# Reordering the transposes of normalized tiles at the end of two output projections, and moving a small parameter copy into an earlier stage

## The chip, the cores and the metric

The kernel runs on one core of one Trainium2 chip. The metric is the device time of one launch, in microseconds (us), as the median of several launches; less is better. The core has five engines, each with its own instruction queue, worked off in order: TensorE (PE, matrix products and transposes), VectorE (DVE), ScalarE (ACT), GpSimd (POOL) and SyncE (SP, which issues nearly all DMAs). They wait for one another only by semaphores.

## The reference, cut to what matters

One sequence of 1024 tokens with 1024 features in float32 goes through two blocks.

```
x = layer_norm(x, ln0)                                     # first block
h = x * (1 + sc_a) + sh_a
y = concat(gated delta rule, gated linear attention)(h) @ w_o
x = layer_norm(ALPHA * x + (1 + gt_a) * y, ln1)            # (A)
h = x * (1 + sc_f) + sh_f
u = causal depthwise conv of 3 taps (h @ w_up) + bias
y = (silu(gate half of u) * value half of u) @ w_down
x = layer_norm(ALPHA * x + (1 + gt_f) * y, ln2)
                                                           # second block
h = x + concat(attention, recurrence)(rmsnorm(x)) @ w_out
h = h + cross_attention(rmsnorm(h)) @ w_co
hid = square(relu(rmsnorm(h) @ w_mlp_in))                  # (B)
out = rmsnorm(h + hid @ w_mlp_out)
```

The change concerns the two places (A) and (B): between the product with `w_o` and the feed-forward, and between the product with `w_co` and the MLP.

## The kernel before, in words

Tokens are cut into 8 tiles of 128 (tile 0 to 7), features into 8 chunks of 128. The function `schedule` (lines 270 to 704) writes one list of steps. Each engine's program walks through this one list and issues its own part of each step, so the list sets the order on every engine at once.

**Output projections.** `grouped_products` multiplies attention output by `w_o` (or `w_co`) for three groups of token tiles, (0,1,2,3), (4,5) and (6,7) (`GROUPS`). A group goes through the panels of the weight, each 256 rows by 512 columns: eight panels for `w_o`, numbered 0 to 7, and four for `w_co`, numbered 0 to 3. Sums stand in the PSUM banks that `GROUP_BANKS` gives. The dictionary `between` is the table that the change edits: the entry (g, n) holds steps that follow panel n of group g. VectorE takes each finished bank: at (A) it multiplies by a gate row and adds to the residual (L1764, L1767), at (B) it adds (L1781).

**Normalization.** `norm_start` computes the statistics of a group: at (A) by VectorE alone (`moments` and `deviation`, L1592 to L1620), at (B) by ScalarE's squares (L2358) and then VectorE's reciprocal root by Newton steps (L1614 to L1620). `norm_apply` writes the normalized tile into one of four buffers `xhat0` to `xhat3` (VectorE L1635 at (A), ScalarE L2367 at (B)). In the kernel these are the lists `a1`, `a2`, `a3` for the three groups.

**Turns.** `norm_features` turns normalized tiles into features-by-tokens: TensorE transposes (L1120) into a PSUM bank, one bank for a chunk, and the bank is emptied into a high part and a low part of the float32 values, which the products of the next stage use. At (A): VectorE scales (L1675) into `feat_part`, ScalarE makes `ft_hi` (L2335), and VectorE (even chunks, L1687) or GpSimd (odd chunks, L2754) makes `ft_lo`. There are only two `feat_part` buffers. At (B): ScalarE makes `ftm_hi` (L2344) and VectorE `ftm_lo` (L1667) straight from the bank. Lists `f1`, `f2`, `f3` hold these steps for the three groups, each entry of a list for two chunks; the third argument of `feats` is the ring of banks that it takes in turn. A transpose waits until its bank has been emptied.

**Around (A).** `rows((4, 5))` multiplies normalized tiles by the gain row (VectorE L1650), after which GpSimd adds the bias row (L2745). Behind group 2 come `ffn_taps` (two copies of convolution parameters and two memsets on VectorE, L1984 to L1989), the `late` steps (the last gate vector: eight products L1096 on TensorE, each with a weight panel of its own), the split of the first three `w_up` panels into high (ACT L2291) and low part (POOL L2679), then `f3`, and then the products of the feed-forward (L1127). ScalarE's first split waits for `rows_applied` of tile 5, since `panel_hi` lies over `xhat0` and `xhat1`:

```
            a.wait_ge(*a.filled("feat", 1, 4, KD - 1))
            a.wait_ge("rows_applied", 1, 5)
```

**Around (B).** `first_panels` splits the first two `w_mlp_in` panels; the MLP begins with columns 0 and 1 for the first half of the tokens, then does all of `f3`, and goes on with column 2.

**Panels.** SyncE loads weight panels of 512 KB into six buffers in list order; a load waits until the buffer's last product is done.

Of the kernel before, what the change touches and what calls it, by code (L numbers as in the profile page):

```python
# [308 lines left out]
def schedule(k):  # L309
# [65 lines left out]
    steps = in_turn([[("delta", n, s) for s in DELTA_STEPS] for n in range(NT)], DELTA_LAG)  # L375
# [9 lines left out]
    for m, (_, n, s) in enumerate(steps):  # L385
        for what in delta_banks(s):
            k.banks.take(("delta", n, *what), (5,) if what == ("o",) else (0, 1, 2, 3, 4))
        k.unit("delta", n, s)
        upto = len(fill) * (m + 1) // len(steps)
        for more in fill[done:upto]:  # L390
            for step in more:
                step()
        done = upto
    k.unit("modulation", 1)
    k.unit("resid_load")
# [12 lines left out]
    def feats(s, tiles, ring):  # L408
        return [lambda c=c: norm_features(k, s, tiles, ring, (c, c + 1)) for c in range(0, KD, 2)]

    def applies(s, tiles):
        return [lambda n=n: norm_apply(k, s, n, tiles) for n in tiles]

    def rows(tiles):
        return [lambda n=n: k.unit("norm_scale_rows", 1, n) for n in tiles]
# [3 lines left out]
    f2, a2 = feats(1, (4, 5), (4, 5)), applies(1, (4, 5))  # L419
    f3, a3 = feats(1, (6, 7), (4, 5)), applies(1, (6, 7))  # L420
    grouped_products(k, "w_o", d["w_o"][0], 8, {
        (0, 7): [lambda: norm_start(k, 1, (0, 1, 2, 3)), *a1],
        (1, 2): f1[0:1], (1, 3): f1[1:2], (1, 4): [f1[2], *rows((0, 1))], (1, 5): [f1[3], *rows((2, 3))],
        (1, 7): [lambda: norm_start(k, 1, (4, 5)), *a2],
        (2, 2): f2[0:1], (2, 3): f2[1:2], (2, 4): f2[2:3], (2, 5): [f2[3], *rows((4, 5))],
        (2, 7): [lambda: norm_start(k, 1, (6, 7)), *a3]})
    w_up, w_down = d["ffn_w_up"][0], d["ffn_w_down"][0]
# [12 lines left out]

    k.unit("ffn_taps")
    for step in late:
# [37 lines left out]
    ring = (4, 5, 6, 7)  # L480
# [121 lines left out]
    ring = (4, 5)  # L602
# [48 lines left out]
    f1, a1 = feats("norm_mlp", (0, 1, 2, 3), ring), applies("norm_mlp", (0, 1, 2, 3))  # L651
    f2, a2 = feats("norm_mlp", (4, 5), ring), applies("norm_mlp", (4, 5))
    f3, a3 = feats("norm_mlp", (6, 7), ring), applies("norm_mlp", (6, 7))
    w_mi, w_mo = d["w_mlp_in_2"][0], d["w_mlp_out_2"][0]
    first_in = []

    def first_panels():
# [4 lines left out]
        (0, 3): [lambda: norm_start(k, "norm_mlp", (0, 1, 2, 3)), *a1],  # L662
        (1, 3): [lambda: norm_start(k, "norm_mlp", (4, 5)), f1[0], f1[1], first_panels],
        (2, 0): f1[2:3], (2, 1): [f1[3], *a2],
        (2, 3): [lambda: norm_start(k, "norm_mlp", (6, 7)), f2[0], f2[1], f2[2], f2[3], *a3]},
        resident=True)
# [857 lines left out]
def vector_program(k):  # L1524
# [458 lines left out]
    def ffn_taps():  # L1983
        dve.tensor_copy(k.ffn_taps[:, :, :, 0:3],  # L1984
                        k.col("ffn_conv", 0, 3 * 2 * NFF).rearrange("p (j g c) -> p g c j", j=3, g=2))
        dve.tensor_copy(k.ffn_taps[:, :, :, 3:4],
                        k.col("ffn_conv_b", 0, 2 * NFF).rearrange("p (g c j) -> p g c j", g=2, j=1))
        for n in range(2):
            m = dve.memset(k.ffn_in[n][:, 0:3], 0.0)  # L1989
        m.then_inc(*v.new("ffn_ready"))  # L1990
# [260 lines left out]
    def mlp_out(i, u, h, p, tiles):  # L2251
        for n in tiles:
            v.wait_ge(*v.filled("mlp_out", i, u, h, n))
            if u or i:
# [7 lines left out]
               norm_features=norm_features, final=final, project=project, to_tokens=to_tokens, decay_gates=decay_gates,  # L2262
               delta_start=delta_start, delta=delta, gla_gates=gla_gates, gla=gla, ffn_taps=ffn_taps, up=up, down=down,
               rg_params=rg_params, rg_in=rg_in, rglru=rglru, angles=angles, masks=masks, score=score, weigh=weigh, merge=merge,
# [822 lines left out]
```

## Time and profile before

| | us |
|---|---|
| median of 3 launches | 3224.68 |
| lowest and highest | 3221.36, 3225.28 |
| launch that was profiled | 3222.75 |
| its span in the trace | 3221.5 |
| TensorE busy in it | 3040.6 |
| VectorE busy | 1491.2 |
| ScalarE busy | 938.2 |
| GpSimd busy | 773.7 |

The launch takes 1.25 us more than the span. Times inside the span count from its start. A row of the timeline reads: start, length, engine, line of the kernel, operation, output and inputs, count; in square brackets how long the engine had been idle before it, and what it waited for.

### The profile page before, as it was taken

The numbers are of one execution on the slowest core, as the hardware profiler recorded it, in microseconds if no ns is written. First come the engines' busy times: TensorE is split into PE (matmuls) and PEld (weight loads), VectorE is DVE, ScalarE is ACT, GpSimd is POOL, SyncE is SP. The second block draws the span as 40 slices with busy tenths as digits, with TensorE's granted clock in tenths as the row PEclk, the third lists the DMA queues.
The fourth block names the chain that finished last, engine by engine and source line by source line (L and its number), as shares of the span: only waits on it lengthen the run. The fifth ranks groups of instructions, "written<-read, shape, count | busy, mean of one in ns | idle before, by whom it ended". The sixth has DMA issues, their size and how long they took to land.

```text
span 3221.5 us, 32486 instructions
## 1 busy us (share of the span) xinstructions
PE 3040.6 (94%) x13068; PEld 2167.0 (67%) x13068; DVE 1491.2 (46%) x2375; ACT 938.2 (29%) x1476; POOL 773.7 (24%) x481
## 2 busy tenths in 40 slices
PE   6999999999979999999997899999998999999997
PEld 3444467675437888888875668785444788888886
DVE  7235443332475554545556564662233333333334
ACT  1236632223012222222224541362243222222123
POOL 3111112211044444444430333111000222222221
PEclk9999999999989999999998999999999999999998
DMA  7210012213231111111113112102201111111111
GB/s 250 66 33 27 27 40 73 65 40 111 87 122 46 60 51 46 46 51 48 46 53 111 33 40 81 60 3 98 93 27 33 39 46 53 46 47 52 46 53 53
DMA packets 199749, 193.55 MB, mean 60 GB/s; under 512 B 16152, under 2 KB 147632, under 8 KB 199600
## 3 DMA queue, kind: packets, MB, share of 16 engines
q1 hardware_dynamic: 197968, 187.09, 18.5%
q10 hardware_dynamic: 1631, 4.40, 0.4%
q8 instruction: 104, 1.70, 0.2%
q14 instruction: 46, 0.37, 0.0%
HBM read 175.43 MB, written 13.89 MB: 59 GB/s over the span
## 4 chain that ended last, share of the span: by engine, by line
PE 82%; DVE 8%; ACT 6%; issue 2%; POOL 1%; DMA 1%; ACTq 0%; SPq 0%; DVEq 0%; POOLq 0%
PE bank L1127 60%; PE bank L1154 6%; PE bank L1450 2%; PE bank L1220 1%; PE bank L1261 1%; PE bank L1120 1%; PE bank L1275 1%; PE bank L1284 1%; PE bank L1434 1%; PE bank L1404 1%; PE bank L1426 1%; PE bank L1096 1%; DVE ffn_conv L2005 1%; DVE ffn_conv L2001 1%; PE bank L1423 1%
## 5 line engine op out<-in xcount | busy, mean ns | idle before, releaser
L1127 PE MATMUL bank<-ft_hi,panel_lo 128*128 128x512 f32 x1216 | 443.8, 398 | 27.9 <-POOL panel_lo L2679 27.9
L2679 POOL TENSOR_TENSOR panel_lo<-panel,panelm_hi 128x1024 fp32r<-128x1024 f32 x64 | 153.3, 2396 | 813.2 <-ACT panelm_hi L2291 813.2
L1127 PEld LDWEIGHTS bank<-ft_hi,panel_lo 128*128 128x128 f32 x1216 | 232.6, 191 | 81.0 <-POOL panel_lo L2679 29.6
L1154 PE MATMUL bank<-ft,panel 128*128 128x512 f32 x576 | 271.5, 609 | 7.4 <-ACT mod_part L2398 4.8
L1127 PE MATMUL bank<-ft_hi,panel_hi 128*128 128x512 f32 x704 | 276.8, 393 | 0.0
L1127 PE MATMUL bank<-ft_lo,panel_hi 128*128 128x512 f32 x704 | 276.4, 393 | 0.0
L2001 DVE TENSOR_SCALAR ffn_conv<-ffn_in,ffn_taps 128x512 f32<-128x512 f32 x88 | 115.5, 1312 | 296.6 <-ACT ffn_in L2538 296.6
L2257 DVE TENSOR_TENSOR resid<-resid,bank 128x512 f32<-128x512 f32 x256 | 174.7, 687 | 151.3 <-PE bank L1127 150.5
L2679 POOL TENSOR_TENSOR panel_lo<-panel,panel_hi 128x1024 fp32r<-128x1024 f32 x66 | 158.5, 2409 | 246.6 <-ACT panel_hi L2291 246.6
L1127 PE MATMUL bank<-ftm_hi,panelm_hi 128*128 128x512 f32 x512 | 201.1, 393 | 0.0
L1127 PE MATMUL bank<-ftm_hi,panel_lo 128*128 128x512 f32 x512 | 200.6, 392 | 0.0
L1127 PE MATMUL bank<-ftm_lo,panelm_hi 128*128 128x512 f32 x512 | 200.6, 392 | 0.0
L1127 PE MATMUL bank<-panelm_hi,mlp_hid_hi 128*128 128x512 f32 x512 | 199.2, 389 | 0.0
L1127 PE MATMUL bank<-panel_lo,mlp_hid_hi 128*128 128x512 f32 x512 | 199.2, 389 | 0.0
L1127 PE MATMUL bank<-panelm_hi,mlp_hid_lo 128*128 128x512 f32 x512 | 199.2, 389 | 0.0
L1154 PEld LDWEIGHTS bank<-ft,panel 128*128 128x128 f32 x576 | 105.3, 194 | 113.9 <-issue 110.7
L1127 PE MATMUL bank<-panel,mix 128*128 128x512 f32 x384 | 169.4, 598 | 2.9 <-DMA panel<-in_w_out 2.0
L2005 DVE SCALAR_TENSOR_TENSOR ffn_conv<-ffn_in,ffn_taps,ffn_conv 128x512 f32<-128x512 f32 x176 | 156.5, 889 | 6.2
L2244 DVE TENSOR_TENSOR mlp_square<-mlp_act 128x512 f32<-128x512 f32 x64 | 44.3, 692 | 236.7 <-ACT mlp_act L2641 236.7
L1127 PEld LDWEIGHTS bank<-ft_lo,panel_hi 128*128 128x128 f32 x704 | 132.7, 189 | 30.9
L1127 PEld LDWEIGHTS bank<-ft_hi,panel_hi 128*128 128x128 f32 x704 | 132.6, 188 | 29.6
L1127 PE MATMUL bank<-panel_hi,ffn_hid_hi 128*128 128x512 f32 x352 | 140.0, 398 | 9.4 <-POOL ffn_hid_lo L2824 6.9
(430 smaller groups left out, 5574.1 us busy)
## 6 DMA issues: line engine op xcount, KB each, us to landing
panel<-in_w_in SPq DMA_DIRECT2D x52, 512.0 KB, 3.7
panel<-in_w_ada SPq DMA_DIRECT2D x48, 512.0 KB, 3.8
panel<-in_ffn_w_up SPq DMA_DIRECT2D x44, 512.0 KB, 3.7
panel<-in_w_mlp_in SPq DMA_DIRECT2D x32, 512.0 KB, 3.9
panel<-in_w_mlp_out SPq DMA_DIRECT2D x32, 512.0 KB, 3.5
panel<-in_w_o SPq DMA_DIRECT2D x24, 512.0 KB, 3.6
panel<-in_w_out SPq DMA_DIRECT2D x24, 512.0 KB, 3.5
panel<-in_ffn_w_down SPq DMA_DIRECT2D x22, 512.0 KB, 3.6
```

The costliest lines, as they stand in the source:

```text
L1096: m = te.matmul(ps[rows, :], k.cond[:, c:c + 1].broadcast_to([P, 32]), w[:, kk, :], start=(c < 4), stop=(c >= 4))
L1120: m = te.transpose(ps[:, tile(i)], src[:, tile(j)], k.ident[:])
L1127: m = te.matmul(ps, a, b, start=(start and j == 0), stop=(stop and j == len(pairs) - 1))
L1154: m = te.matmul(ps[:], w[0][:, kk, :], k.ft[:, kk, half(h)], start=(kk == 0), stop=(kk == KD - 1))
L1220: m = te.matmul(ps[:, tile(h)], lhs(h), rhs_of(h), start=True, stop=True)
L1261: m = te.matmul(ps[:, h * GC:(h + 1) * GC], t.ltm[:, h, :], blocks(t.inv, lv, 0)[:, h], start=True, stop=True)
L1450: m = te.matmul(ps[:, at:at + HD + 1], k.p_t[(2 * t + hb) % 4][:, 2 * side + c, :], v, start=(hb == side == c == 0), stop=(hb == side == c ...
L2001: dve.tensor_scalar(out, pre[:, 1 + h * BANK:1 + (h + 1) * BANK], w[:, 0:1], w[:, 3:4], ALU.mult, ALU.add).then_inc(*v.new("ffn_tap", c, g ...
L2005: dve.scalar_tensor_tensor(out, pre[:, 1 + j + h * BANK:1 + j + (h + 1) * BANK], w[:, j:j + 1], out, ALU.mult, ALU.add).then_inc(*v.new("f ...
L2244: dve.tensor_tensor(k.mlp_sq[h][:], k.mlp_act[h][:], k.mlp_act[h][:], ALU.mult).then_inc(*v.new("mlp_square", i, c, h))
L2257: evict(dve.tensor_tensor(r, r, v.bank("mlp_out", i, u, h, n)[:], ALU.add), "mlp_out", i, u, h, n)
L2679: pool.tensor_tensor(lo, k.view(p), hi.bitcast(F32), ALU.subtract).then_inc(*g.new("halved_lo", p))
```

## The change

The steps stay the same; their places in the list, the banks of some, and the place of one copy change.

- (A), group 2 (tiles 6 and 7): the four steps of `f2` (the turns of tiles 4 and 5) stood behind panels 2, 3, 4 and 5, and now stand behind 4, 5 and 6 (two steps behind 6). `rows((4, 5))` stood behind panel 5 and now stands behind `a3`, the normalization of tiles 6 and 7.
- (A), `f3`: eight banks in turn in place of banks 4 and 5.
- (A), the two copies into `ffn_taps` are made in the middle of the delta rule; the two memsets stay, as `ffn_edges`.
- (B), group 1: the first two steps of `f1` stood behind panel 3 and behind the statistics of tiles 4 and 5; now the first stands behind panel 2, the second behind panel 3 and ahead of those statistics.
- (B), group 2: `f2` stood behind panel 3 and behind the statistics of tiles 6 and 7; now two steps stand behind panel 2 and two behind panel 3, ahead of those statistics. Its ring has four banks in place of two, `f3` has eight.

```diff
+        if m == len(steps) // 2:
+            k.unit("ffn_taps")
...
-    f3, a3 = feats(1, (6, 7), (4, 5)), applies(1, (6, 7))
+    f3, a3 = feats(1, (6, 7), tuple(range(8))), applies(1, (6, 7))
...
-        (2, 2): f2[0:1], (2, 3): f2[1:2], (2, 4): f2[2:3], (2, 5): [f2[3], *rows((4, 5))],
-        (2, 7): [lambda: norm_start(k, 1, (6, 7)), *a3]})
+        (2, 4): f2[0:1], (2, 5): f2[1:2], (2, 6): f2[2:4],
+        (2, 7): [lambda: norm_start(k, 1, (6, 7)), *a3, *rows((4, 5))]})
...
-    k.unit("ffn_taps")
+    k.unit("ffn_edges")
...
-    f2, a2 = feats("norm_mlp", (4, 5), ring), applies("norm_mlp", (4, 5))
-    f3, a3 = feats("norm_mlp", (6, 7), ring), applies("norm_mlp", (6, 7))
+    f2, a2 = feats("norm_mlp", (4, 5), (2, 3, 4, 5)), applies("norm_mlp", (4, 5))
+    f3, a3 = feats("norm_mlp", (6, 7), tuple(range(8))), applies("norm_mlp", (6, 7))
...
-        (1, 3): [lambda: norm_start(k, "norm_mlp", (4, 5)), f1[0], f1[1], first_panels],
-        (2, 0): f1[2:3], (2, 1): [f1[3], *a2],
-        (2, 3): [lambda: norm_start(k, "norm_mlp", (6, 7)), f2[0], f2[1], f2[2], f2[3], *a3]},
+        (1, 2): f1[0:1], (1, 3): [f1[1], lambda: norm_start(k, "norm_mlp", (4, 5)), first_panels],
+        (2, 0): f1[2:3], (2, 1): [f1[3], *a2], (2, 2): f2[0:2],
+        (2, 3): [f2[2], f2[3], lambda: norm_start(k, "norm_mlp", (6, 7)), *a3]},
```

On TensorE in group 2 of the product with `w_o`, the order before was this (`mixed` and `g_v` hold attention output, `xhat0` and `xhat1` the normalized tiles 4 and 5, `ident` the identity; a panel shows as two banks, two products each):

```order
L1127 MATMUL bank6<-panel0_79,mixed_90 128x512 x2
L1127 MATMUL bank7<-panel0_79,mixed_90 128x512 x2
L1120 MATMUL bank4<-ident_49,xhat0_153 128x128
L1120 MATMUL bank4<-ident_49,xhat1_154 128x128
L1120 MATMUL bank5<-ident_49,xhat0_153 128x128
L1120 MATMUL bank5<-ident_49,xhat1_154 128x128
L1127 MATMUL bank0<-panel1_80,mixed_90 128x512 x2
```

In the changed kernel, from the same panel on:

```order
L1129 MATMUL bank6<-panel0_79,mixed_90 128x512 x2
L1129 MATMUL bank7<-panel0_79,mixed_90 128x512 x2
L1129 MATMUL bank0<-panel1_80,mixed_90 128x512 x2
L1129 MATMUL bank1<-panel1_80,mixed_90 128x512 x2
L1129 MATMUL bank6<-panel2_81,g_v_92 128x512 x2
L1129 MATMUL bank7<-panel2_81,g_v_92 128x512 x2
L1122 MATMUL bank4<-ident_49,xhat0_153 128x128
L1122 MATMUL bank4<-ident_49,xhat1_154 128x128
```

Two panels now stand between the second panel-half and the first transpose of tile 4.

On VectorE behind the normalization of tiles 6 and 7 (`xhat_155`, `xhat_156`) at (A), before:

```order
L1635 TENSOR_SCALAR xhat_155<-resid,moments,rstd 128x1024
L1635 TENSOR_SCALAR xhat_156<-resid,moments,rstd 128x1024
L1984 COPY ffn_taps<-cols 128x44x3
L1986 COPY ffn_taps<-cols 128x44
L1989 MEMSET ffn_in_170 128x3
L1989 MEMSET ffn_in_171 128x3
L1561 SCALAR_TENSOR_TENSOR gate_row<-bank,gate_row 128x512 x2
L1675 TENSOR_SCALAR feat_part_157<-bank,in_scale,in_bias 128x256
```

and in the changed kernel:

```order
L1637 TENSOR_SCALAR xhat_155<-resid,moments,rstd 128x1024
L1637 TENSOR_SCALAR xhat_156<-resid,moments,rstd 128x1024
L1652 TENSOR_TENSOR resid<-xhat_153,norm_rows 128x1024
L1652 TENSOR_TENSOR resid<-xhat_154,norm_rows 128x1024
L1993 MEMSET ffn_in_170 128x3
L1993 MEMSET ffn_in_171 128x3
L1563 SCALAR_TENSOR_TENSOR gate_row<-bank,gate_row 128x512 x2
L1677 TENSOR_SCALAR feat_part_157<-bank,in_scale,in_bias 128x256
```

The two copies are gone from here, and the rows of tiles 4 and 5 have come in their place.

On ScalarE at (B), behind the normalization of tiles 0 to 3 (`square` are the squares of tiles 4 and 5, `panelm_hi` the split of the MLP's first panels), before:

```order
L2367 ACTIVATE xhat3_156<-resid2_205,rstd_61 128x1024
L2358 ACTIVATE square_159,moments_60<-resid2_205 128x1024 x2
L2344 ACTIVATE ftm_hi_238<-bank4,cols_52 128x512
L2344 ACTIVATE ftm_hi_238<-bank5,cols_52 128x512
L2344 ACTIVATE ftm_hi_238<-bank4,cols_52 128x512
L2344 ACTIVATE ftm_hi_238<-bank5,cols_52 128x512
L2291 ACTIVATE panelm_hi0_248<-panel0_79 128x1024
```

and in the changed kernel:

```order
L2371 ACTIVATE xhat3_156<-resid2_205,rstd_61 128x1024
L2348 ACTIVATE ftm_hi_238<-bank4,cols_52 128x512
L2348 ACTIVATE ftm_hi_238<-bank5,cols_52 128x512
L2348 ACTIVATE ftm_hi_238<-bank4,cols_52 128x512
L2348 ACTIVATE ftm_hi_238<-bank5,cols_52 128x512
L2362 ACTIVATE square_159,moments_60<-resid2_205 128x1024 x2
L2295 ACTIVATE panelm_hi0_248<-panel0_79 128x1024
```

The squares, and VectorE's Newton steps that wait for them, now stand behind the first four chunks.

## Rows read from the trace of the kernel before

**Rows 1.** The page: chain that ended last, share of the span by engine.

```profile
PE 82%; DVE 8%; ACT 6%; issue 2%; POOL 1%; DMA 1%; ACTq 0%; SPq 0%; DVEq 0%; POOLq 0%
```

**Rows 2.** Chain that ended last, in order of time: start, us, what.

```profile
954.65 18.63 PE bank L1127 x72
...
1025.81 620.60 PE bank L1127 x2688
...
2515.08 676.45 PE bank L1127 x2976
```

**Rows 3.** Waits of TensorE at (A): line, waited for, total, times, longest.

```profile
PE bank L1120 <- DVE xhat L1635: 7.2, 6, 5.7
PE bank L1120 <- DVE feat_part L1675: 6.0, 4, 5.1
```

**Rows 4.** Timeline of TensorE at (A), 897 to 955 us.

```profile
897.39 5.42 PE L1127 MATMUL bank<-panel,mixed 128*128 128x512 f32 x12 [0.70 <-DVE gated L1764]
908.54 0.45 PE L1120 MATMUL bank<-ident,xhat 128*128 128x128 f32 x1 [5.73 <-DVE xhat L1635]
...
916.08 3.60 PE L1127 MATMUL bank<-panel,g_v 128*128 128x512 f32 x8
...
919.95 3.60 PE L1127 MATMUL bank<-panel,g_v 128*128 128x512 f32 x8
...
930.78 2.77 PE L1096 MATMUL bank<-panel,cond 128*32 128x512 f32 x20
...
941.76 1.99 PE L1108 MATMUL bank<-mod_last,quads 128*128 128x512 f32 x2 [0.74 <-ACT mod_last L2398]
...
954.30 0.78 PE L1127 MATMUL bank<-ft_hi,panel_hi 128*128 128x512 f32 x1
```

**Rows 5.** Timeline of VectorE at (A), 925 to 948 us.

```profile
925.17 2.88 DVE L1650 TENSOR_TENSOR resid<-xhat,norm_rows 128x1024 f32<-128x1024 f32 x2
...
928.70 2.12 DVE L1767 TENSOR_TENSOR resid<-resid,gated 128x512 f32<-128x512 f32 x1
...
936.57 1.28 DVE L1592 BATCH_NORM_STATS2 stats<-resid 128x6 f32<-128x512 f32 x2
...
941.89 1.53 DVE L1635 TENSOR_SCALAR xhat<-resid,moments,rstd 128x1024 f32<-128x1024 f32 x2
943.34 2.39 DVE L1984 COPY ffn_taps<-cols 128x132 f32<-128x132 f32 x1
945.65 2.35 DVE L1986 COPY ffn_taps<-cols 128x44 f32<-128x44 f32 x1
```

**Rows 6.** Timeline of GpSimd at (A), 926 to 951 us.

```profile
926.94 6.11 POOL L2745 TENSOR_TENSOR resid<-resid,norm_rows 128x1024 f32<-128x1024 f32 x2
942.74 7.50 POOL L2679 TENSOR_TENSOR panel_lo<-panel,panel_hi 128x1024 fp32r<-128x1024 f32 x3 [9.69 <-ACT panel_hi L2291]
```

**Rows 7.** Timeline of VectorE in the delta rule, around 612 us.

```profile
611.97 0.69 DVE L1895 TENSOR_TENSOR rhs<-bank,g_col 128x512 f32<-128x512 f32 x1 [2.61 <-PE bank L1220]
```

**Rows 8.** Waits of TensorE, 2400 to 2560 us.

```profile
PE bank L1120 <- DVE ftm_lo L1667: 14.5, 7, 4.5
```

**Rows 9.** Timeline of TensorE at (B).

```profile
2465.45 1.97 PE L1120 MATMUL bank<-ident,xhat 128*128 128x128 f32 x8 [4.30 <-DVE ftm_lo L1667]
...
2489.68 1.11 PE L1120 MATMUL bank<-ident,xhat 128*128 128x128 f32 x4 [4.47 <-DVE ftm_lo L1667]
```

**Rows 10.** Chain that ended last, at (B).

```profile
2472.72 0.88 PE bank L1120 x8
2473.59 3.44 PE bank L1127 x8
...
2494.48 12.80 PE bank L1127 x48
```

**Rows 11.** Timeline of ScalarE at (B).

```profile
2450.93 4.27 ACT L2367 ACTIVATE xhat<-resid,rstd 128x1024 f32<-128x1024 f32 x4 [2.42 <-DVE rstd L1620]
...
2522.43 0.60 ACT L2641 ACTIVATE mlp_act<-bank 128x512 f32<-128x512 f32 x1 [6.84 <-PE bank L1127]
```

More of the change, by code:

```diff
@@ L1987, in ffn_taps, with ffn_edges @@
                         k.col("ffn_conv_b", 0, 2 * NFF).rearrange("p (g c j) -> p g c j", g=2, j=1))
+    def ffn_edges():
         for n in range(2):
@@ L2262, in vector_program @@
                norm_features=norm_features, final=final, project=project, to_tokens=to_tokens, decay_gates=decay_gates,
-               delta_start=delta_start, delta=delta, gla_gates=gla_gates, gla=gla, ffn_taps=ffn_taps, up=up, down=down,
+               delta_start=delta_start, delta=delta, gla_gates=gla_gates, gla=gla, ffn_taps=ffn_taps, ffn_edges=ffn_edges, up=up, down=down,
                rg_params=rg_params, rg_in=rg_in, rglru=rglru, angles=angles, masks=masks, score=score, weigh=weigh, merge=merge,
```

## The prediction

> **What bounds the kernel now.** I read the chain that ended last first, since it says which engine's work a microsecond must be taken from. TensorE holds 82% of it [rows 1], so the kernel gets shorter where TensorE waits, or where it runs slowly behind a wait. In order of time the chain shows two long stretches on which nothing but products lie, 620.60 us from 1025.81 and 676.45 us from 2515.08 [rows 2]. What comes ahead of each is a seam: (A), from the product with `w_o` to 1025.81, and (B), from the product with `w_co` to 2515.08. The waits then say what TensorE lacks there. At (A) its transposes wait 7.2 us for normalized tiles (one wait of 5.7) and 6.0 us for the emptying of banks 4 and 5 (one of 5.1) [rows 3]; at (B) they wait 14.5 us for the emptying of the same two banks, 4.5 the longest [rows 8]. The timelines place them: 5.73 us ahead of 908.54, 4.30 ahead of 2465.45, 4.47 ahead of 2489.68 [rows 4, 9]. Work behind a wait is slower too: at 2489.68 four transposes take 1.11 us, and the first feed-forward product takes 0.78 us [rows 4, 9]; in the stretches of rows 2 one product takes 620.60 / 2688 = 0.231 us.
>
> **(A), group 2 on TensorE.** The second and third panel of the group end at 897.39 + 5.42 = 902.81, then comes the wait of 5.73 for tiles 4 and 5 and the group ends at 930.78 [rows 4]. Five panels were left. In the changed kernel two of them stand ahead of the first transpose, 2 x 3.44 us, until 909.7; the normalized tiles come at about 909.1 as before, so the wait goes. A panel and its four transposes take 919.95 - 916.08 = 3.87 us [rows 4]: 5 x 3.44 + 4 x 0.43 = 18.9 us. One gap is new. The last two steps of `f2` stand together, and their two banks are emptied only after VectorE has done two tiles of panel 6 (four operations of 0.7 us, begun during the panel); I put it at 1.6 us. The group ends at 902.8 + 20.5 = 923.3, 7.5 us earlier.
>
> **(A), VectorE.** Now the statistics of tiles 6 and 7 begin at 936.57, 5.8 us behind the group's end, since `rows((4, 5))` (2.88 us) goes ahead and its partner on GpSimd (6.11 us for two) slows the first additions behind it from 0.7 to 2.12 us [rows 5, 6]. With the rows moved behind, I count on VectorE from the end of panel 6 (917.5): two tiles 1.4 more us, the last four chunks of `f2` to 922.6, and four operations on the last two tiles, the last of which starts 1.2 us behind the group's end: statistics at 925.6, 11.0 us earlier. From there the start of the feed-forward follows from a chain on VectorE and GpSimd: 943.42 - 936.57 = 6.85 us until both tiles are normalized, 1.44 until the row of tile 4 is done, 6.1 for the two additions on GpSimd (with VectorE's operations between), 2.5 for the first low part of a `w_up` panel (7.50 / 3) [rows 5, 6]. Sum 16.9, so 942.5 against 954.30 [rows 4], 11.8 us. The other things that this product needs come earlier: the late gate vector's last product on TensorE ended at 943.75, 13.0 us behind the group's end [rows 4], so now at 936.3, and the eight banks let all of `f3`'s transposes follow it in 2 us. I take off 0.8 for a stretch at half clock that the new gap of 1.6 us may bring (it would cost 8 x 0.2 us): **11 us**, between 8 and 13.
>
> The rest of `f3` gains less. GpSimd makes three low parts ahead of its share of `f3`: they end at 942.5 + 2 x 2.5 = 947.5 against 942.74 + 7.50 = 950.24 now [rows 6], so `f3` ends only 2.7 us earlier. Its end now is near 957, by four pairs of chunks at 1.7 us behind 950.24 (two features, a low part on each engine), so 954.5 in the changed kernel. The third unit of the feed-forward is the first to use it. Three units took from 954.30 to 954.65 + 18.63 = 973.3 [rows 2, 4], the third 24 x 0.231 = 5.5, so it starts 13.5 us behind the first, at 956. I see `f3` covered, but the cover is thin: 1.5 us. The chain passes through the end of this third unit [rows 2], which shifts with TensorE.
>
> **The copies.** They take 2.39 and 2.35 us now, for 132 and 44 elements, while GpSimd makes three low parts in 7.50 us [rows 5, 6]; 44 elements cannot cost as much as 132 by their own work, so it is the waiting for GpSimd that I read there. In the delta rule they stand ahead of two operations that end a 2.61 us idle time before [rows 7]. Between nothing and 4.7 us, I take 0.5 us of VectorE work and nothing on the path. If that cover were gone, 2.1 us would be lost. The Trainium skill says in "SBUF — State Buffer", section "SBUF: two separate sides", that VectorE and GpSimd hold a shared port pair exclusively for a whole instruction; the trace agrees with the 2.39 and 2.12 us. It speaks against moving the rows next to the splits: were the two engines free of each other, the 6.1 us would be about 4.5 and the start 1.5 us earlier, and that is no term of the sum.
>
> **(B).** TensorE has ended panel 3 of group 1 and eight transposes at 2465.45 - 4.30 = 2461.15, so panel 2 at 2461.15 - 0.88 - 3.44 = 2456.8 [rows 9, 10]. Tiles 0 to 3 are normalized at 2455.2 [rows 11], so the first turn no longer waits. What is left until the first MLP product is five panels of 3.44, four pairs of chunks of four tiles at 0.88, and four pairs of two tiles at 0.43 [rows 10]: 17.2 + 3.5 + 1.7 = 22.4, which gives 2479.2 against 2494.48 [rows 10]: 15.3 us. For this ScalarE must keep step. From 2461.5, when the second pair of chunks is turned, it has two high parts, two squares, two splits, four high parts and two normalizations ahead of the turn of tiles 4 and 5: six operations over 1024 elements at 4.27 / 4 = 1.07 us and six over 512 at 0.60 to 0.70 [rows 11], 10.0 to 10.6 us, and some 1.5 us in which it waits for TensorE's fourth pair. That ends near 2473.6, and the transposes are due at 2456.8 + 17.2 = 2474.0: 0.4 us of room.
>
> Behind it 48 products took 12.80 us [rows 10], and 48 x 0.231 = 11.1 without a wait ahead: 1.6 us. The turns of tiles 6 and 7 took 2507.3 to 2515.08, 7.8 us; on eight banks the 16 transposes need 1.8, and the next unit's bank is empty 1.5 us later: 4.5 us. That unit took until 2522.4 [rows 11], 7.3 us against 24 x 0.231 = 5.6: 1.7 us. Sum 15.3 + 1.6 + 4.5 + 1.7 = **23 us**, between 15 and 25. From there TensorE alone is on the path [rows 2], so all of it counts.
>
> **Sum.** 3222.75 - 11 - 23 = 3188.8 for the profiled launch, which was 1.9 us below the median of the three. I predict 3190.
>
> **Rivals.**
> 1. As above, 3183 to 3195: chance 0.60.
> 2. At (A) the feed-forward's start follows `f3` and the conversions behind it, not TensorE: only 3 us are gained there. For it: the cover of 1.5 us. Against it: the chain now runs through TensorE's first three units, 18.63 us without a gap [rows 2], not through `f3`. 3222.75 - 3 - 23 = 3197: 0.13.
> 3. At (B) ScalarE comes late for tiles 4 and 5, and a wait like that of 2465.45 returns: 4.3 us, and 3.0 us of slow work behind it (2472.72 - 2465.45 = 7.3 for what takes 0.88 + 3.44 at full speed [rows 9, 10]). For it: 0.4 us of room. 3189 + 7 = 3196: 0.14.
> 4. The turns wait all the same, now for other banks or for panels, and the two seams keep their length: 3220 to 3224. Against it: every load follows a product, so loads move with TensorE. 0.05.
> 5. Slower: the transposes now stand in closer company and TensorE is granted half clock for long behind them. A product then costs 0.2 us more (0.43 against 0.231); the forecast's 34 us are used up after 170 such products, seven units at the feed-forward's start, and past 200 it is slower. Against it: behind 954.30 only some ten products were slow. Above 3229: 0.03.
> The last 0.05 lies between these, mostly at smaller gains.
>
> **Numbers.** From 3183 (13 and 25 us) to 3201 holds 1, 2, 3 and a little more: 8 in 10 or above. A measurement of this kernel tells about 0.2%, 6.4 us, from no change. Faster by more: 1, 2, 3 and most of the rest, 0.92; within: 0.05; slower: 0.03.
>
> **What would show it.** Right: no wait of 5.7 us for `xhat` in group 2, statistics of tiles 6 and 7 near 925.6, first feed-forward product near 942.5, the 620 us stretch starting near 1015, first MLP product 15 us earlier in relation to the start of `w_co`'s product, waits of L1120 for `ftm_lo` near 1.5 us in place of 14.5, granted clock 1.00 from 2460 to 2500. Wrong: a wait of L1127 for `ft_lo` or `ftm_hi` at either start, a longer gap on VectorE near 608, or TensorE waiting for `xhat` after panel 2 of group 2 at (B).

## The result and the profile after

The changed kernel took 3196.36 us (median of four launches, 3190.62 to 3199.6), the kernel before 3223.75 beside it (four, 3221.36 to 3225.28): a ratio of 0.9913, 95% interval 0.9901 to 0.9924, or 27.4 us less. The forecast was 3190, from 3183 to 3201. The measured time lies in the range, but 6 us above the forecast, so a term was too large. The launches that were profiled took 3222.75 and 3196.19 us, 26.6 less.

In the rows of after, line numbers are 2 to 4 higher. The chain that ended last shows where the two seams end now, to be held against [rows 2]:

```profile
1012.77 622.76 PE bank L1129 x2688
...
2488.51 676.46 PE bank L1129 x2976
```

The first long stretch of products begins 13.0 us earlier, takes 2.2 us longer, the part between the stretches takes 1.0 us longer, and the last one begins 26.6 us earlier. The product with `w_co` began at 2418.84 and now begins at 2408.99, so 16.7 us of it come from seam (B) and 9.9 are left of (A). The forecast had 11 for (A) and 23 for (B).

**(A).** Waits of TensorE from 905 to 1021 us in the changed kernel, the first three rows (line, waited for, total, times, longest). The waits of 5.7 and 5.1 us in [rows 3] are gone; the largest is new, one for GpSimd:

```profile
PE bank L1129 <- POOL panel_lo L2683: 4.0, 1, 4.0
PE bank L1129 <- ACT ffn_in L2542: 3.5, 2, 3.3
PE bank L1098 <- DMA panel<-in_w_ada: 2.9, 3, 1.2
```

Timeline of TensorE there, answering to [rows 4]:

```profile
895.66 8.85 PE L1129 MATMUL bank<-panel,mixed 128*128 128x512 f32 x20 [0.71 <-DVE gated L1766]
...
917.66 0.89 PE L1122 MATMUL bank<-ident,xhat 128*128 128x128 f32 x4 [1.53 <-DVE feat_part L1677]
918.39 3.60 PE L1129 MATMUL bank<-panel,g_v 128*128 128x512 f32 x8
921.92 2.77 PE L1098 MATMUL bank<-panel,cond 128*32 128x512 f32 x20
...
933.52 2.04 PE L1122 MATMUL bank<-ident,xhat 128*128 128x128 f32 x16
939.58 0.80 PE L1129 MATMUL bank<-ft_hi,panel_hi 128*128 128x512 f32 x1 [4.02 <-POOL panel_lo L2683]
```

The 16 transposes of tiles 6 and 7 stand together. Then TensorE waits 4.02 us for the first low part. Why that is late stands in the timeline of GpSimd:

```profile
931.44 5.60 POOL L2749 TENSOR_TENSOR resid<-resid,norm_rows 128x1024 f32<-128x1024 f32 x2 [10.22 <-DVE resid L1652]
936.99 7.21 POOL L2683 TENSOR_TENSOR panel_lo<-panel,panel_hi 128x1024 fp32r<-128x1024 f32 x3
```

The high parts came from ScalarE at 932.61 to 934.8, but GpSimd first had the two additions for tiles 4 and 5. VectorE, answering to [rows 5]:

```profile
923.36 1.28 DVE L1594 BATCH_NORM_STATS2 stats<-resid 128x6 f32<-128x512 f32 x2
...
928.69 1.53 DVE L1637 TENSOR_SCALAR xhat<-resid,moments,rstd 128x1024 f32<-128x1024 f32 x2
930.14 2.35 DVE L1652 TENSOR_TENSOR resid<-xhat,norm_rows 128x1024 f32<-128x1024 f32 x2
```

The copies, in the delta rule, answering to [rows 7]: 0.23 and 0.20 us in place of 2.39 and 2.35. Idle time still follows them, 2.39 us where it was 2.61.

```profile
608.30 0.23 DVE L1986 COPY ffn_taps<-cols 128x132 f32<-128x132 f32 x1
608.45 0.20 DVE L1988 COPY ffn_taps<-cols 128x44 f32<-128x44 f32 x1
...
611.94 0.69 DVE L1897 TENSOR_TENSOR rhs<-bank,g_col 128x512 f32<-128x512 f32 x1 [2.39 <-PE bank L1222]
```

**(B).** Waits of TensorE, 2380 to 2540 us. The 14.5 us of [rows 8] are gone, and three new waits, 5.8 us in all, have come:

```profile
PE bank L1122 <- DVE ftm_lo L1669: 2.8, 1, 2.8
PE bank L1129 <- DVE ftm_lo L1669: 2.4, 1, 2.4
...
PE bank L1122 <- ACT mlp_act L2645: 0.6, 1, 0.6
```

Their places in the timeline of TensorE: the fourth step of `f1` (the second turn of [rows 9] had waited 4.30 us), the last turn of `f3`, and the third MLP unit.

```profile
2462.71 1.31 PE L1122 MATMUL bank<-ident,xhat 128*128 128x128 f32 x8 [2.79 <-DVE ftm_lo L1669]
...
2485.66 0.44 PE L1122 MATMUL bank<-ident,xhat 128*128 128x128 f32 x2 [0.57 <-ACT mlp_act L2645]
2488.51 0.60 PE L1129 MATMUL bank<-ftm_hi,panelm_hi 128*128 128x512 f32 x1 [2.41 <-DVE ftm_lo L1669]
```

What held the low part up is on VectorE, in the root steps for tiles 4 and 5:

```profile
2456.38 0.16 DVE L1622 SCALAR_TENSOR_TENSOR rstd<-newton,rstd 128x2 f32<-128x2 f32 x1
2456.57 2.21 DVE L1620 SCALAR_TENSOR_TENSOR newton<-rstd 128x2 f32<-128x2 f32 x1
2458.82 2.27 DVE L1621 TENSOR_TENSOR newton<-newton 128x2 f32<-128x2 f32 x1
2461.12 0.16 DVE L1622 SCALAR_TENSOR_TENSOR rstd<-newton,rstd 128x2 f32<-128x2 f32 x1
...
2482.02 2.43 DVE L2248 TENSOR_TENSOR mlp_square<-mlp_act 128x512 f32<-128x512 f32 x1 [3.76 <-ACT mlp_act L2645]
```

Two operations on two elements per partition take 2.2 us where their like take 0.16. GpSimd's timeline has one instruction of 2.35 us beside each, and one beside `mlp_square`:

```profile
2456.37 4.70 POOL L2683 TENSOR_TENSOR panel_lo<-panel,panelm_hi 128x1024 fp32r<-128x1024 f32 x2 [259.62 <-ACT panelm_hi L2295]
2481.52 2.39 POOL L2683 TENSOR_TENSOR panel_lo<-panel,panelm_hi 128x1024 fp32r<-128x1024 f32 x1 [20.46 <-ACT panelm_hi L2295]
```

In the kernel before, GpSimd's first pair of low parts began at 2469.17, after the root steps had ended at 2464.6; now the step of `f1` with its 1.41 us of low parts is queued on VectorE behind them.

### The profile page after: what moved, and what is told of

Its sections match the earlier page's. It is cut to its first block, busy times and chain, and to the rows that moved or that the text cites. A ratio compares the mean times of both kernels' runs of the same rounds, so it can differ in the third digit from the quotient of the medians.

```text
span 3195.0 us, 32486 instructions
## 1 busy us (share of the span) xinstructions
PE 3023.4 (95%) x13068; PEld 2157.7 (68%) x13068; DVE 1488.9 (47%) x2375; ACT 936.3 (29%) x1476; POOL 771.9 (24%) x481
## 4 chain that ended last, share of the span: by engine, by line
PE 82%; DVE 7%; ACT 6%; POOL 2%; issue 1%; DMA 1%; SPq 0%; ACTq 0%; DVEq 0%; POOLq 0%
PE bank L1129 60%; PE bank L1156 6%; PE bank L1452 2%; PE bank L1222 1%; PE bank L1263 1%; PE bank L1277 1%; PE bank L1286 1%; PE bank L1436 1%; PE bank L1406 1%; DVE ffn_conv L2009 1%; PE bank L1428 1%; PE bank L1098 1%; POOL panel_lo L2683 1%; PE bank L1122 1%; PE bank L1425 1%
## 5 line engine op out<-in xcount | busy, mean ns | idle before, releaser
L2005 DVE TENSOR_SCALAR ffn_conv<-ffn_in,ffn_taps 128x512 f32<-128x512 f32 x88 | 114.0, 1295 | 289.5 <-ACT ffn_in L2542 289.5
L1129 PE MATMUL bank<-panel_hi,ffn_hid_hi 128*128 128x512 f32 x352 | 141.6, 402 | 10.9 <-POOL ffn_hid_lo L2828 6.9
```

The lines of the kernel that those rows point to most:

```text
L1129: m = te.matmul(ps, a, b, start=(start and j == 0), stop=(stop and j == len(pairs) - 1))
L2005: dve.tensor_scalar(out, pre[:, 1 + h * BANK:1 + (h + 1) * BANK], w[:, 0:1], w[:, 3:4], ALU.mult, ALU.add).then_inc(*v.new("ffn_tap", c, g ...
```

## The experiments

Since launches of one kernel differ by up to 9 us, I read each experiment in its trace by three distances besides its median. **S**: from the last turn of `f2` at (A) (917.66 in the changed kernel) to the first feed-forward product. **L**: from the same turn to the long product stretch. **B**: from the start of the product with `w_co` to the end of the last product stretch (before: 2515.08 + 676.45 - 2418.84 = 772.7).

| kernel | median | ratio to before, 95% | S | L | B |
|---|---|---|---|---|---|
| changed | 3196.36 | 0.9913 (0.9901, 0.9924) | 21.9 | 95.1 | 756.0 |
| a_only | 3211.26 | 0.9958 (0.9945, 0.9970) | 21.7 | 95.1 | 772.5 |
| b_only | 3207.52 | 0.9945 (0.9932, 0.9957) | | | 757.4 |
| taps_back | 3195.55 | 0.9906 (0.9891, 0.9921) | 22.1 | 95.4 | 757.4 |
| rows_back | 3197.56 | 0.9915 (0.9902, 0.9929) | 27.2 | 97.6 | 756.1 |
| splits_late | 3190.44 | 0.9900 (0.9885, 0.9914) | 21.9 | 95.1 | 749.6 |
| splits_early | 3191.36 | 0.9904 (0.9889, 0.9918) | 21.9 | 95.1 | 752.7 |
| adds_late | 3194.20 | 0.9911 (0.9894, 0.9927) | 18.5 | 94.6 | 756.1 |
| third_bank | 3189.75 | 0.9899 (0.9884, 0.9914) | 21.9 | 95.1 | 751.2 |
| f3a_two | 3200.60 | 0.9931 (0.9917, 0.9944) | 30.1 | 100.6 | 757.4 |
| f3b_two | 3198.84 | 0.9925 (0.9912, 0.9937) | 21.9 | 95.1 | 760.0 |
| best1 | 3186.23 | 0.9887 (0.9873, 0.9900) | 21.7 | 95.1 | 747.8 |
| best2 | 3181.36 | 0.9870 (0.9857, 0.9883) | 18.5 | 91.9 | 747.8 |

S and L stand only for kernels with the new order at (A), since in the old one the last turn of `f2` has another place. Where nothing was changed at the seam, they repeat there within 0.3 us. The old order repeats less well: from the row that ends the wait for `gated` (897.39 in [rows 4], 895.66 in the changed kernel) to the long stretch it is 128.4 us in the kernel before and 129.3 in b_only, and 117.1 in the changed kernel and in a_only. The change at (A) is thus worth 11.3 to 12.2 us up to the long stretch. B takes one of two values where (B) is that of the changed kernel, 756.0 or 757.4: in the second kind the eight transposes behind the wait of 2.9 us took 1.97 us and not 1.31 (granted clock 0.50 from 2470.40 to 2472.40 in b_only, 1.00 from 2462.60 to 2464.00 in the changed kernel).

**The two halves apart.** a_only has the changes at (A) and the copies, b_only those at (B).

> The changes at (A) and the copies alone, (B) as before. Theory (the two seams add up, and what (A) gained is 11.3 us less 1.4 lost in the long product stretch): 10 us under before, about 3213, with the first feed-forward product near 940 and everything from the product with w_co on as in before, shifted. Rival (the gain at (A) is given back in the feed-forward or in the second block when (B) waits as before): within 4 us of before, 3219 or more.

> The changes at (B) alone. Theory (VectorE's small root steps wait for GpSimd's low parts of the first two MLP panels, and that costs the predicted gain its missing part): 16 to 17 us under before, about 3206, with a wait of 2 to 3 us of TensorE for ftm_lo at the fourth turn of group 1 as in the changed kernel. Rival (the shortfall at (B) comes from the other phase in which (A) leaves the loads and the clock): 21 to 23 us under before, about 3200.

Measured: 12.9 and 16.7 us under before (3224.19 beside them). L and B are those of the changed kernel in the half that was changed, and B is that of before in a_only. In b_only TensorE waits 2.94 us for `ftm_lo` at the fourth turn, as expected. The rivals fall: the two seams are independent, and what (B) lacks it lacks by itself.

**The copies.** The unit stands again where it was, behind the rows of tiles 4 and 5:

```diff
-        if m == len(steps) // 2:
-            k.unit("ffn_taps")
...
+    k.unit("ffn_taps")
     k.unit("ffn_edges")
```

> The changed kernel, with the two copies of the convolution parameters back ahead of the two memsets, so behind the rows of tiles 4 and 5 on VectorE and beside GpSimd's additions. Theory: each copy is held until a GpSimd instruction ends, 2.2 to 2.8 us for each, but the first feed-forward product waits for GpSimd's low part and not for VectorE, so the start stays near 939.6 and the time within 2 us of the changed kernel. Rival (the copies were on the path of the start, as the sum of the prediction allowed): the start 4 to 5 us later, time about 3201.

Measured: the first copy took 0.23 us and only the second was held, for 2.40 us, so the theory's "each copy" was wrong. S and L grew by 0.2 us only, and the median is that of the changed kernel. The rest of the theory holds: VectorE's 2.4 us lie in TensorE's wait for GpSimd. Moving the copies is worth next to nothing here.

**The rows of tiles 4 and 5**, ahead of the statistics again:

```diff
-        (2, 4): f2[0:1], (2, 5): f2[1:2], (2, 6): f2[2:4],
-        (2, 7): [lambda: norm_start(k, 1, (6, 7)), *a3, *rows((4, 5))]})
+        (2, 4): f2[0:1], (2, 5): f2[1:2], (2, 6): [*f2[2:4], *rows((4, 5))],
+        (2, 7): [lambda: norm_start(k, 1, (6, 7)), *a3]})
```

> The changed kernel, with the rows of tiles 4 and 5 (VectorE's products and GpSimd's additions) behind the last step of f2 in group 2, ahead of the statistics of tiles 6 and 7. Theory A (rows ahead of the statistics delay the start by 4 us, as the prediction counted): statistics near 927.5, first feed-forward product 2 to 4 us later than 939.6, time 3198 to 3200. Theory B (the start waits for GpSimd's low part, which waits for GpSimd's additions of the rows; with the additions done earlier the low part is ready near 936): first product near 937.5, 2 us earlier, time about 3194, with TensorE waiting for xhat instead.

Measured: the start is 5.2 us later, more than either theory gave. The statistics came at 929.72, 10.9 us behind the last turn and not 5.7, 5.2 us later where theory A counted 4. Behind them the root steps fell beside GpSimd's low parts, which started at 934.28. The timeline of VectorE in rows_back:

```profile
934.45 2.20 DVE L1620 SCALAR_TENSOR_TENSOR newton<-rstd 128x2 f32<-128x2 f32 x1
936.68 2.27 DVE L1621 TENSOR_TENSOR newton<-newton 128x2 f32<-128x2 f32 x1
938.98 2.26 DVE L1622 SCALAR_TENSOR_TENSOR rstd<-newton,rstd 128x2 f32<-128x2 f32 x1
```

GpSimd's low parts did begin earlier, as theory B wanted (15.5 us behind the last turn and not 19.3), but now TensorE waits 7.81 us for `xhat`. Three root steps were held ahead of `xhat`, which is the thing that the forecast missed at (B). Of the 5.2 us, L keeps 2.4. The median moved by 1.2 us, less than launches differ, so this one stands on the trace alone.

**The splits of the first MLP panels**, moved to either side of the root steps. splits_late:

```diff
-        k.unit("ahead", used=first_in[0])
...
-        (2, 0): f1[2:3], (2, 1): [f1[3], *a2], (2, 2): f2[0:2],
+        (2, 0): [f1[2], lambda: k.unit("ahead", used=first_in[0])], (2, 1): [f1[3], *a2], (2, 2): f2[0:2],
```

splits_early:

```diff
-        (1, 2): f1[0:1], (1, 3): [f1[1], lambda: norm_start(k, "norm_mlp", (4, 5)), first_panels],
+        (1, 2): [first_panels, f1[0]], (1, 3): [f1[1], lambda: norm_start(k, "norm_mlp", (4, 5))],
```

> The changed kernel, with the splits of the first MLP panels moved behind the third step of f1 (entry (2, 0)), so that GpSimd's low parts begin after VectorE's small root steps for tiles 4 and 5; the third panel's split comes with them, ahead of the turn of tiles 6 and 7. Theory (the root steps waited for GpSimd's low parts): root steps 2.4 us in all instead of 6.3, no wait of 2.8 us of TensorE for ftm_lo at the fourth turn, first MLP product 2.8 us earlier, and up to 1.4 us more at the third MLP unit, since mlp_square takes 0.7 and not 2.4 us: 3 to 4 us under the changed kernel, about 3192. Rival (ScalarE is what is late: squares, splits and high parts in its queue): now one more split stands ahead of the high parts of the fourth turn, the wait stays or grows to 3 us: 3196 or more.

> The changed kernel, with the splits of the first two MLP panels ahead of the first step of f1 (entry (1, 2)), where ScalarE was idle for 2.1 us, and the loads of the four panels in the same place. GpSimd's low parts then lie from 2446.4 to 2451.1, beside VectorE's additions and low parts, which read a bank, and ahead of the root steps. Theory (only operations of VectorE with both inputs in SBUF wait for GpSimd, as 0.7 us for operations with a bank beside GpSimd's instructions at (A) suggest): no wait at the fourth turn, 2.8 us earlier, about 3193. Rival (operations that read a bank wait for GpSimd too): the low parts of the first step come 2 to 4 us late, TensorE waits at the second turn instead, no gain: 3196.

Measured: B is 6.4 and 3.3 us shorter, the medians 5.9 and 5.0 under the changed kernel. In both, the wait at the fourth turn is gone. splits_late puts three splits ahead of the high parts of that turn on ScalarE and does not wait for them, so ScalarE was not what was late. splits_late gains more since the third panel's split has moved too: `mlp_square` takes 0.69 us and not 2.43, TensorE waits 1.6 us ahead of the third MLP unit and not 2.41 (2.4 in splits_early), and the granted clock from 2490 to 2495 is 1.00 where it was 0.79. The row of VectorE and the wait of TensorE in splits_late:

```profile
2480.41 0.69 DVE L2248 TENSOR_TENSOR mlp_square<-mlp_act 128x512 f32<-128x512 f32 x1 [2.81 <-ACT mlp_act L2645]
```

```profile
PE bank L1129 <- DVE ftm_lo L1669: 1.6, 1, 1.6
```

In splits_early VectorE works beside GpSimd's low parts (row of GpSimd, then two of VectorE):

```profile
2445.04 4.68 POOL L2683 TENSOR_TENSOR panel_lo<-panel,panelm_hi 128x1024 fp32r<-128x1024 f32 x2 [249.32 <-ACT panelm_hi L2295]
```

```profile
2446.95 1.41 DVE L1669 SCALAR_TENSOR_TENSOR ftm_lo<-bank,cols,ftm_hi 128x512 fp32r<-128x512 f32 x2 [0.55 <-ACT ftm_hi L2348]
2448.31 0.69 DVE L1783 TENSOR_TENSOR resid<-resid,bank 128x512 f32<-128x512 f32 x1
```

They take what they take alone, 0.7 us for each: an operation that reads a bank is not held in any of these rows. The rival of splits_early falls. Its theory is too narrow, though. Two inputs in SBUF are not what it takes: the copies of [rows 5] have one, and so have the first convolution steps (`ffn_conv`, L2005 of the changed kernel, a TENSOR_SCALAR of 512 elements with one tap for each partition), which took 0.54 us alone at 952.46 and 2.23 us at 1004.93, where GpSimd had an instruction of 2.39 us from 1004.48. What the held operations have in common is that they read no bank; whether every such operation is held, no run tells.

**The third MLP unit's bank.** third_bank turns the last two chunks of `f3` behind the third unit:

```diff
-                for step in ((), f3, ())[c]:
+                for step in ((), f3[0:3], f3[3:4])[c]:
```

> The changed kernel, with the last step of f3 at (B) (chunks 6 and 7) behind the third MLP unit in place of ahead of it, so that this unit finds an empty bank and needs not wait until f3's first bank is emptied. Theory (the wait of 2.4 us ahead of the third unit is for a bank): that wait goes, and what comes in its place is at most the last two chunks, turned while ScalarE has had 5.5 us: 2 us under the changed kernel, about 3194. Rival (the wait only moves behind the third unit, since f3's high and low parts end no earlier): the fourth unit waits as long, no change, 3196.

Measured: B is 4.8 us shorter, the median 6.6 lower, more than the 2 expected. The wait of 2.4 us is gone and the one of 0.57 for `mlp_act` with it. The rest is the clock: busy time by stretches of 5 us (stretch, length, busy time and instructions of the engines, granted clock PEclk), first the changed kernel, then third_bank.

```profile
2485.00:2490.00 5.00, 2.03 (x7) 1.43 (x7) 4.12 (x9) 4.00 (x11) 0.00 (x0) 0.87 0.00 0
2490.00:2495.00 5.00, 5.00 (x19) 3.97 (x19) 1.10 (x3) 0.15 (x1) 0.00 (x0) 0.79 0.01 3
```

```profile
2485.00:2490.00 5.00, 5.00 (x25) 4.15 (x24) 3.50 (x8) 3.14 (x9) 0.00 (x0) 1.00 0.01 3
2490.00:2495.00 5.00, 5.00 (x23) 4.13 (x22) 1.98 (x4) 1.33 (x3) 0.00 (x0) 1.00 0.03 5
```

Without idle time in front the clock stays at 1.00, and the second stretch holds 23 instructions in place of 19. Idle time need not bring it down either: it stayed at 1.00 behind the 1.6 us of splits_late. The 4.8 us less the 3.0 of the two waits leave 1.8 us, which I put down to the clock.

**GpSimd's additions at (A).** adds_late takes them out of the wait for the first low part:

```diff
-        if n < 6:
+        if n < 4:
             rows_add(s, (n,))
...
-    k.unit("rows_add", 1, (6, 7))
+    k.unit("rows_add", 1, (4, 5))
     for n in range(2):
         up(0, n, first[n], 1)
+    k.unit("rows_add", 1, (6, 7))
```

> The changed kernel, with GpSimd's additions of the bias row to tiles 4 and 5 behind the first two units of the feed-forward, and those to tiles 6 and 7 behind the fourth; VectorE's order is the same. Theory (the first feed-forward product waits for GpSimd's low part, and this for the two additions of 5.6 us, while the high parts are ready at 933.7): low parts from 933.7, first product near 936.3, 3.3 us earlier; 2 to 3 us under the changed kernel, about 3193. Rival (the additions, now beside the first convolutions, hold up VectorE there, as one pair did already with 5.59 us for two operations): the gain is lost again at the units behind, 3196 or more.

Measured: S is 3.4 us shorter, as expected, but L only 0.5, and the ratio to before is no different (0.9911 beside 0.9913). The rival holds. The second pair lies beside VectorE's convolutions at 975.98. In the chain of adds_late two convolution steps are held there, where the changed kernel has 2.78 and 0.76:

```profile
978.70 2.79 DVE ffn_conv L2010
981.51 2.77 DVE ffn_conv L2010
```

The step behind them took 1.37 us for 0.56, so the three account for 2.8 of the 2.9 us that were given back.

**The eight banks, one seam at a time** (f3a_two: `(4, 5)` for `tuple(range(8))` in `f3` at (A); f3b_two: `ring` at (B)).

> The changed kernel, with f3 at (A) on banks 4 and 5 again. Theory (between the start of the feed-forward and the long product stretch the path runs through f3's conversions and VectorE's convolutions, so the eight banks count there): in the kernel before, f3 ended near 957 and in the changed one near 951; with two banks TensorE's transposes also stand ahead of the first product, so that the start follows the emptying: start 4 to 7 us later than in the changed kernel, the long stretch 3 to 6 us later, time 3199 to 3202. Rival (the eight banks do nothing here, since the low part of the panel comes at the same time): start within 1 us of 22 us behind the last turn of group 2, time about 3196.

> The changed kernel, with f3 at (B) on the old ring of two banks. Theory (the prediction's term for the eight banks, 4.5 us, was right): the turns take about 7.8 us in place of the 2.8 until the third unit's wait of 2.4, time 3 to 4.5 us over the changed kernel, about 3200. Rival (ScalarE's high parts set the pace with two banks as with eight): within 1 us of the changed kernel.

Measured: at (A) S grows by 8.2 us and L by 5.5, the median by 4.2; at (B) B grows by 4.0 and the median by 2.5. Both theories hold, with a start that is later than the 4 to 7 us of the first and a median that moved less than the 3 to 4.5 us of the second. Waits of TensorE, first in f3a_two from 905 us, then in f3b_two from 2440 us:

```profile
PE bank L1122 <- DVE feat_part L1677: 11.9, 6, 4.5
```

```profile
PE bank L1122 <- DVE ftm_lo L1669: 8.6, 4, 4.4
```

**Together.** best1 is splits_early with third_bank. best2 adds the additions, the second pair this time behind the first half of the first product with `w_down`:

```diff
                 down(i, h, ps[h], tiles)
+                if i == 0 and h == 0:
+                    k.unit("rows_add", 1, (6, 7))
```

> splits_early and third_bank together. Theory (the wait of 2.9 at the fourth turn and the one of 2.4 ahead of the third MLP unit are apart from each other): both go, 5.3 us under the changed kernel in the trace from the product with w_co to the long MLP stretch; time about 3190 to 3191 beside 3196 for the changed kernel. Rival (they cover each other: the MLP begins earlier, but tiles 6 and 7 are normalized no earlier, so a wait for xhat takes their place): 3192 or more.

> best1, with GpSimd's additions of the bias row to tiles 4 and 5 behind the first two feed-forward units (as in adds_late) and those to tiles 6 and 7 behind the first half of the first product with w_down. In adds_late the start came 3.4 us earlier, and 2.9 of it were given back where the second pair of additions lay beside VectorE's convolutions. Theory (in this stretch VectorE and GpSimd work one after the other, so only work taken out of it counts): the gain of 3 us stays, long stretch 3 us earlier in relation to the last turn of group 2, time 3187 to 3188. Rival (the additions delay GpSimd's low parts of the next panels, or VectorE's emptying of the banks for tiles 6 and 7 waits for them): no gain over best1 or a loss of up to 5 us.

Measured: 3186.23 and 3181.36 us, 10 and 15 under the changed kernel, with intervals of the ratio apart from its own (0.9873 to 0.9900 and 0.9857 to 0.9883 against 0.9901 to 0.9924). At (B) TensorE waits for nothing from 2440 to 2560 in either, and B is 8.2 us shorter: in best1 3.2 up to the first MLP product, as in the two kernels with moved splits, and 4.9 behind it, as in third_bank. That is more than the 5.3 of the two waits, and I put the rest down to the wait of 0.57 and to the clock, as in third_bank. In best2 the first feed-forward product and the pair of additions lie so (TensorE, then GpSimd):

```profile
936.41 0.50 PE L1131 MATMUL bank<-ft_hi,panel_hi 128*128 128x512 f32 x1 [1.05 <-POOL panel_lo L2685]
```

```profile
1013.12 4.77 POOL L2751 TENSOR_TENSOR resid<-resid,norm_rows 128x1024 f32<-128x1024 f32 x2
```

Both S and L are 3.2 to 3.4 us shorter: with the additions behind the start of the long stretch at 1009.80, the gain at the start is kept. The medians of best1 and best2 lie 4.9 us apart, but the intervals of their ratios overlap; the 3.2 us in L are what the traces show.

## Why the prediction was right, and what was off

**(A), 11 us: right.** To compare it with the rows, 1.7 us come off first: the changed kernel was already that much ahead at the row of 895.66 (before: 897.39, [rows 4]), in a part whose order the change doesn't touch. There the granted clock was 0.85 from 866 to 872 us and 0.80 from 872 to 876 before, and 1.00 in both in the changed kernel. Predicted and measured, the latter with 1.7 added:

- End of group 2: 923.3, measured 923.6. The gap of 1.6 us is there, at 1.53.
- Statistics of tiles 6 and 7: 925.6, measured 925.1.
- First product: 942.5, measured 941.3.
- Long stretch: near 1015, measured 1014.5, so 11.3 us earlier (13.0 with the 1.7). Of the 13.0, 9.9 arrive at the start of (B): the stretch itself took 2.2 us more, as in best1 (622.79 for 620.6) and in no other run by more than 0.5, and the part behind it 1.0. That 1.0 is not the change's: from the end of the long stretch to the product with `w_co` it is 772.4 us in the trace of before, and at least 773.3 in every other, b_only with its old (A) among them. So the 9.9 is not the worth of (A): 1.7 us that the clock gave ahead of it are in it, and 3.2 us were lost in parts whose order the change leaves alone.
- The copies: nothing on the path, as predicted.

The working was less right than the sum. It took the start as TensorE's and `f3` as a thing thinly covered. In the chain of the changed kernel, no TensorE work lies between 949.7 and 1011.9 but VectorE's rows and convolutions, with ScalarE's and GpSimd's pieces between them. Where that stretch begins:

```profile
948.84 0.55 DVE feat_part L1677
949.39 0.33 DVE ft_lo L1689
949.72 0.67 DVE resid L1652
```

f3a_two shows that the banks of `f3` alone carry 5.5 us there, which the prediction didn't price at (A). That is the mechanism of rival 2. It took no gain away since `f3` ended 4.7 us earlier and not 2.7 (its last low part on GpSimd began at 949.91 + 1.7 = 951.6, before at 956.34): GpSimd began its own share of `f3` at 944.16 + 1.7 = 945.9, where the prediction had 947.5, and eight banks then let nothing else wait. That (A) came out at 11 is in part luck, then: of the 11.3 us, f3a_two gives 5.5 to the banks, rows_back 2.4 to the place of the rows and taps_back 0.2 to the copies. If these add up, some 3 us are left for the later turns of `f2`, an estimate that no run checks by itself.

**(B), 23 us: 16.7 measured, the term that was mis-sized.**

- 15.3 for the order of the turns, measured 11.9 (first MLP product 2472.40 - 2408.99 = 63.4 us behind the start of the product with `w_co`, before 2494.13 - 2418.84 = 75.3). The step that failed is the condition under this term, "For this ScalarE must keep step", with its 0.4 us of room: it named ScalarE as the only engine that the turns could wait for. ScalarE did keep step. What the sum left out is VectorE's root steps, which the change put beside GpSimd's low parts. In splits_early and in splits_late, without that, the product comes at 60.2 us, and 60.4 was predicted (2479.2 - 2418.84). So the price of the held root steps is 3.2 us, and 1.3 to 1.5 us more where the clock falls behind the wait (64.9 us in b_only, taps_back and f3a_two). Rival 3 had a wait for `ftm_lo` come back, as it did, but for the turns of tiles 4 and 5 and through ScalarE; it was the last turn of tiles 0 to 3, through VectorE. Its 3196 is the measured time by luck.
- 1.6 and 4.5 for the first units and `f3`, measured 4.8 (from the first product to the third unit 20.95 before, 16.1 now). The 1.6 is 12.80 - 11.1, so 1.7 by its own rows. The wait ahead of the third unit was to be 1.5 us and was 0.57 + 2.41, since `mlp_square` was held for 2.43 us; in splits_late, where it was not, that wait is 1.6. The eight banks are worth 4.0, by f3b_two.
- 1.7 for the third unit at full clock, measured 0: it stood behind idle time again, and the clock was 0.87 and 0.79. third_bank gets it.

The Trainium skill says in "SBUF — State Buffer", section "SBUF: two separate sides", that a VectorE operation with two inputs in SBUF, against a GpSimd instruction that reads SBUF, or one in a 2-port performance mode, can't run beside GpSimd, and that whichever starts first keeps the ports for its whole length. The rows agree for 2.21, 2.27 and 2.43 us, for the 0.69 us of the operations with a bank, and for the copies and convolution steps with one input, though no run here shows in which mode those ran. The prediction used this rule for the rows at (A) and did not go through VectorE's queue with it at (B).

Of the signs that the prediction named for being right, two did not come: the waits of L1120 for `ftm_lo` were to be near 1.5 us and are 2.8 at the turns and 2.4 ahead of the third unit, and the granted clock from 2485 to 2495 is 0.87 and 0.79 and not 1.00. Rivals 4 and 5 did not come: the old waits are gone, and no long half clock follows.

## What to carry to other kernels

When work is moved, write down what stands on VectorE and on GpSimd at the same moment, and count each VectorE operation that reads no bank as up to one whole GpSimd instruction, however small it is. Work of GpSimd belongs beside operations that read banks, or beside a stretch in which VectorE has time. A gain at the start of a stage counts only up to the next place where these two engines take turns, so read the chain to the end of the seam and not to its first product. If a unit needs just one bank, leave one out of the turns ahead of it.

## What was not expected of the hardware

An operation on 128x2 elements, 0.16 us alone, took 2.20 to 2.27 us beside a GpSimd instruction, three times in a row in rows_back. And the clock differs from launch to launch in code that is the same: the same idle time of 2.9 us (2.79 to 2.95) was followed by eight transposes in 1.31 us in five traces and in 1.97 in three. The last turn of `f2` began between 916.9 and 920.3 us in the twelve traces in which it has the same place. That such a spread comes from the clock was looked at for one pair only, before and the changed kernel (0.85 and 0.80 against 1.00 from 866 to 876 us, 1.7 us), and is not shown for the others. Two profiles of this kernel can't be compared by their totals to better than some 2 us; distances inside a seam repeat to 0.3 us at (A) in the new order, to 0.9 in the old one, and to 1.4 at (B).
